# Attention probabilities turned by transposing DMAs instead of TensorE transposes, with some products of values moved later

## The reference, cut to what matters

```
s = einsum('bqhd,bkhd->bhqk', q, k) * scale        # scores, masked
p = softmax(s, axis=-1)
y = einsum('bhqk,bkhd->bqhd', p, v)                # product of values
```

## Time and profile before

| | us |
|---|---|
| median of 3 runs | 1520.27 (1520.24 to 1520.3) |
| the profiled execution | 1520.18 |
| its span, first to last instruction | 1518.1 |
| TensorE busy | 1510.1 |
| VectorE busy | 637.6 |
| ScalarE busy | 475.0 |
| GpSimd busy | 1027.0 |

### The profile page before, as it was taken

The page is one execution under the profiler, slowest core; times in us unless marked ns, Lnnn a source line. Parts: engine busy times, 40 slices in busy tenths (PEclk is TensorE's granted clock), DMA queues, the critical chain, the costliest instruction groups (busy, mean ns, idle before and its releaser), DMA issues.

```text
span 1518.1 us, 32667 instructions
## 1 busy us (share of the span) xinstructions
PE 1510.1 (99%) x13880; PEld 1174.1 (77%) x13882; DVE 637.6 (42%) x1509; ACT 475.0 (31%) x1243; POOL 1027.0 (68%) x565
## 2 busy tenths in 40 slices
PE   9999999999999999999999999999999999999998
PEld 7666888898666866669889966669888889888885
DVE  4332385445332333315844533325454535464532
ACT  3221163413221132204541232213443313343322
POOL 6976667667767677775586677773858565648653
PEclk9999999999999999999999999999999999999999
DMA  9665554455655565555545465664455554546551
GB/s 390 224 212 200 183 189 173 167 179 217 210 200 198 192 237 207 194 202 196 175 167 186 176 236 194 204 211 156 161 198 193 183 195 155 177 150 239 170 192 56
DMA packets 42625, 293.96 MB, mean 194 GB/s; under 512 B 4720, under 2 KB 5232, under 8 KB 8688
## 3 DMA queue, kind: packets, MB, share of 16 engines
q1 hardware_dynamic: 41760, 290.83, 54.5%
q10 hardware_dynamic: 720, 1.04, 0.2%
HBM read 290.81 MB, written 1.05 MB: 192 GB/s over the span
## 4 chain that ended last, share of the span: by engine, by line
PE 97%; DVE 2%; ACT 1%; issue 0%; DVEq 0%
PE ps L774 26%; PE ps L656 15%; PE ps L657 15%; PE ps L658 15%; PE ps L775 13%; PE ps L675 1%; PE ps L677 1%; PE ps L676 1%; PE ps L869 1%; PE ps L889 1%; ACT ps L1308 1%; PE ps L823 0%; PE ps L734 0%; PE ps L824 0%; PE ps L825 0%; PE ps L851 0%
## 5 line engine op out<-in xcount | busy, mean ns | idle before, releaser
L626 POOL TENSOR_TENSOR w_low<-ring 128x1024 f16<-128x1024 f32 (+1 forms) x544 | 1008.2, 1880 | 379.0 <-DMA ring<-in_w 378.7
L656 PE MATMUL ps<-hP,ring 128*128 128x256 f16 (+1 forms) x1936 | 469.1, 257 | 0.8 <-DVE work L1957 0.4
L657 PE MATMUL ps<-hP,ring 128*128 128x256 f16 (+1 forms) x1936 | 468.9, 257 | 0.0
L658 PE MATMUL ps<-hP,w_low 128*128 128x256 f16 (+1 forms) x1936 | 468.8, 257 | 0.0
L774 PE MATMUL ps<-hP,ring 128*128 128x512 f16 x1280 | 416.3, 380 | 0.0
L775 PE MATMUL ps<-hP,w_low 128*128 128x256 f16 x1280 | 349.2, 273 | 0.0
L774 PEld LDWEIGHTS ps<-hP,ring 128*128 128x128 bf16 x1280 | 125.0, 98 | 151.5 <-issue 0.4
L656 PEld LDWEIGHTS ps<-hP,ring 128*128 128x128 bf16 x1936 | 189.9, 98 | 23.3 <-issue 5.4
L657 PEld LDWEIGHTS ps<-hP,ring 128*128 128x128 bf16 x1936 | 189.2, 98 | 15.6
L658 PEld LDWEIGHTS ps<-hP,w_low 128*128 128x128 f16 x1936 | 189.2, 98 | 15.5
L774 PE MATMUL ps<-work,ring 128*128 128x512 f16 x528 | 171.8, 380 | 0.0
(11 more groups left out here) (277 smaller groups left out, 1740.8 us busy)
## 6 DMA issues: line engine op xcount, KB each, us to landing
ring<-in_w SPq DMA_DIRECT2D x261, 1024.0 KB, 4.8
ring<-in_w SPq DMA_DIRECT2D x12, 512.0 KB, 3.6
con<-in_const SPq DMA_DIRECT2D x1, 2812.0 KB, 18.3
gm<-in_gm SPq DMA_DIRECT2D x2, 1024.0 KB, 17.8
ring<-in_w SPq DMA_DIRECT2D x2, 768.0 KB, 4.9
ring<-in_w SPq DMA_DIRECT2D x2, 560.0 KB, 5.4
ring<-in_w SPq DMA_DIRECT2D x2, 544.0 KB, 3.5
xT<-in_x SPq DMA_DIRECT2D x3, 256.0 KB, 4.1
```

Of the source, the lines that this page charges most:

```text
L626: nc.gpsimd.tensor_tensor(w_low[:, c % SLOTS, a:b], ring[:, c % SLOTS, a:b], w_high[:, c % SLOTS, a:b], ALU.subtract).then_inc(split.by((c ...
L656: nc.tensor.matmul(bank, w_high[:, slot, a:a + m], rhs(k, 0), start=(k == 0), stop=False)
L657: nc.tensor.matmul(bank, w_high[:, slot, a:a + m], rhs(k, 1), start=False, stop=False)
L658: mm = nc.tensor.matmul(bank, w_low[:, slot, a:a + m], rhs(k, 0), start=False, stop=(k == kt - 1))
```

## The change: what it does

`normalise` writes the rounded 16-bit probabilities straight into `probsP` (head, high or low part, column) in SBUF. A new function `lows` on VectorE forms the low parts from PSUM by eight instructions, one per head and half of the queries, and raises `probs_ready` after every two heads. `turn` moves from TensorE to ScalarE's queue: for each two heads it waits for `probs_ready` and issues one transposing DMA from `probsP` to `probsTP`, both parts at once. TensorE's 12 transposes per unit, `copy_turned` and `low_turned` go, with the semaphores `turned`, `turned_copied` and `turned_low`. `mix` waits for the two DMAs of its unit.

In the second mixers the product of "s" moves behind bk0 to bk3 and bv0, bv1; that of "w" behind kcmp, vcmp and merge(0,0), and the scores of "b" behind one more merge; the product of "b" moves on by two merge tiles in all. All later steps of these mixers keep their order and stand two merge tiles further on, up to the stick-breaking product, and the last stage's turn of the stream is one tile later. On ScalarE and VectorE the same steps move along; dk1 is taken ahead of the exponentials of "w" and ahead of the last `rope`.

```diff
+        probsP = work[:, 0:4 * PACK].bitcast(F16).rearrange("p (h s n) -> p h s n", h=4, s=2)
...
-                def turn(s, u):
-                    pe.wait_ge(*probs_ready.at((s, u)))
-                    for h in range(4):
-                        for a in range(0, PACK, P):
-                            mm = nc.tensor.transpose(ps[:, 4 + h, a:a + P], probs[:, h, a:a + P], const("ident"))
-                    mm.then_inc(turned.by((s, u)), 1)
...
-                    pe.wait_ge(*turned_low.at((s, u)))
+                    pe.wait_ge(probs_turned, 32 * in_turn[s, u])
...
-                    turn(s, "s")
                     gemm("dq", 1), gemm("dk", 0)
-                    mix(s, "s", "cvg", lambda t, h: c_vg_h[:, t, 0:HD], lambda t, h: c_vg_l[:, t, 0:HD])
                     for n in range(4):
                         gemm("bk", n)
                     gemm("bv", 0), gemm("bv", 1)
+                    mix(s, "s", "cvg", lambda t, h: c_vg_h[:, t, 0:HD], lambda t, h: c_vg_l[:, t, 0:HD])
...
-                    turn(s, "w")
                     gemm("hid", 0), gemm("hid", 1), gemm("dg", 1)
-                    mix(s, "w", "cvg", lambda t, h: c_vg_h[:, t, HD:P], lambda t, h: c_vg_l[:, t, HD:P])
                     gemm("kcmp", 0), gemm("vcmp", 0)
                     merge(0, 0)
+                    mix(s, "w", "cvg", lambda t, h: c_vg_h[:, t, HD:P], lambda t, h: c_vg_l[:, t, HD:P])
+                    merge(0, 1)
                     pe.wait_ge(*mixed_taken.at((s, "w")))
                     pe.wait_ge(*taken(s, ("bq", 3)))
                     scores(s, "b", lambda h: b_qT[:, h, :], lambda h: b_kT[:, h, :])
-                    merge(0, 1), merge(0, 2), merge(0, 3)
-                    turn(s, "b")
-                    merge(0, 4), merge(0, 5)
+                    for n in range(2, 8):
+                        merge(0, n)
                     mix(s, "b", "bv", lambda t, h: b_v_h[:, t, h * HD:h * HD + HD],
                         lambda t, h: b_v_l[:, t, h * HD:h * HD + HD])
-                    merge(0, 6)
+                    merge(1, 0)
...
-                def copy_turned(s, u):
-                    act.wait_ge(*turned.at((s, u)))
-                    nc.scalar.activation(probsTP[:, :, 0, :], ps[:, 4:8, 0:PACK], ACT.Copy).then_inc(turned_copied.by((s, u)), 1)
+                def turn(s, u):
+
+                    for half in range(2):
+                        act.wait_ge(*probs_ready.at((s, u, half)))
+                        hs = slice(2 * half, 2 * half + 2)
+                        act.dma_start_transpose(probsTP[:, hs, :, :].rearrange("p h s (a q) -> p (h s a) q", q=P),
+                                                probsP[:, hs, :, :].rearrange("p h s n -> p (h s n)")).then_inc(probs_turned, 16)
...
-                        ins = nc.vector.tensor_tensor(probs[:, :, a:b], ps[:, 4:8, a:b], r, ALU.mult)
-                    ins.then_inc(probs_ready.by((s, u)), 1)
-
-                def low_turned(s, u):
-                    dve.wait_ge(*turned_copied.at((s, u)))
-                    nc.vector.tensor_tensor(probsTP[:, :, 1, :], ps[:, 4:8, 0:PACK], probsTP[:, :, 0, :], ALU.subtract
-                                            ).then_inc(turned_low.by((s, u)), 1)
+                        ins = nc.vector.tensor_tensor(probsP[:, :, 0, a:b], ps[:, 4:8, a:b], r, ALU.mult)
+                    chain.link(ins)
+
+                def lows(s, u):
+                    for h in range(4):
+                        for t, (a, b) in enumerate(HALVES):
+                            ins = nc.vector.scalar_tensor_tensor(probsP[:, h, 1, a:b], ps[:, 4 + h, a:b], sums[:, t, h:h + 1],
+                                                                 probsP[:, h, 0, a:b], ALU.mult, ALU.subtract)
+                        if h % 2:
+                            ins.then_inc(probs_ready.by((s, u, h // 2)), 1)
```

More of the change, by code:

```diff
@@ L479, in build @@
         exps_ready = signal("exps_ready", units)
[L480 to L483, removed]
+        probs_ready = signal("probs_ready", [(s, u, half) for s, u in units for half in range(2)])
+        in_turn = {unit: i + 1 for i, unit in enumerate(units)}
         v_split = signal("v_split", [(s, u) for s in mixers for u in (("v",) if s in MIX_A else ("av", "cvg", "bv"))])
@@ L1141, in mixer_b @@
                     mm.then_inc(cmp_turned.by(s), 1)
-                    merge(1, 1)
+                    merge(1, 3)
                     pe.wait_ge(*cmp_copied.at(s))
@@ L1148, in mixer_b @@
                     mm.then_inc(cmp_mixed.by(s), 1)
-                    merge(1, 2)
+                    merge(1, 4)
                     pe.wait_ge(*y_low.at((s, "c")))
@@ L1155, in mixer_b @@
                     mm.then_inc(stick_scores.by(s), 1)
-                    for n in range(3, 8):
+                    for n in range(5, 8):
                         merge(1, n)
-                    merge(2, 0)
+                    merge(2, 0), merge(2, 1), merge(2, 2)
                     pe.wait_ge(*stick_low.at(s))
@@ L1169, in mixer_b @@
                     mm.then_inc(stick_sums.by(s), 1)
-                    merge(2, 1), merge(2, 2), merge(2, 3)
+                    merge(2, 3), merge(2, 4), merge(2, 5)
                     pe.wait_ge(*stick_probs.at(s))
                     mix_values(lambda t, h: d_v[:, t, h * HD:h * HD + HD]).then_inc(stick_mixed.by(s), 1)
-                    for p in range(20, 32):
-                        if s == LAST_STAGE and p == 22:
+                    for p in range(22, 32):
+                        if s == LAST_STAGE and p == 23:
                             pe.wait_ge(*y_low.at((s, "d")))
@@ L1378, in mixer_a @@
                     take("va", 0)
-                    copy_turned(s, 0)
+                    turn(s, 0)
                     take("va", 1)
@@ L1385, in mixer_a @@
                         take("ga", n)
-                    copy_turned(s, 1)
+                    turn(s, 1)
                     act.wait_ge(*variance.at(s))
@@ L1494, in mixer_b @@
                     gate("ag", 0)
-                    copy_turned(s, "a")
+                    turn(s, "a")
                     gate("ag", 1)
@@ L1503, in mixer_b @@
                     take("dq", 0)
-                    copy_turned(s, "s")
+                    turn(s, "s")
                     take("dq", 1)
@@ L1535, in mixer_b @@
                     nc.scalar.activation(ps[:, 4:8, 0:PACK], ps[:, 4:8, 0:PACK], ACT.Ln, bias=1.0).then_inc(stick_ln.by(s), 1)
-                    for p in range(12, 18):
-                        if p == 15:
+                    for p in range(14, 20):
+                        if p == 17:
                             act.wait_ge(*stick_sp.at(s))
@@ L1542, in mixer_b @@
                     nc.scalar.activation(probsT, ps[:, 4:8, 0:PACK], ACT.Exp).then_inc(stick_probs.by(s), 1)
-                    merge(2, 2), merge(2, 3)
+                    merge(2, 4), merge(2, 5)
                     y_parts(3)
-                    for p in range(20, 24):
-                        if s == LAST_STAGE and p == 22:
+                    for p in range(22, 24):
+                        if s == LAST_STAGE and p == 23:
                             for i in range(4):
@@ L1863, in mixer_a @@
                     normalise(s, 0)
-                    low_turned(s, 0)
+                    lows(s, 0)
                     y_parts(0)
@@ L1874, in mixer_a @@
                     normalise(s, 1)
-                    low_turned(s, 1)
+                    lows(s, 1)
                     dve.wait_ge(*deviation.at(s))
@@ L2026, in mixer_b @@
                     low("qc", 1), low("kc", 0)
+                    lows(s, "a")
                     for t in range(TT):
@@ L2040, in mixer_b @@
                     normalise(s, "s", gates_c(1))
+                    lows(s, "s")
                     gate("bg", 1)
@@ L2080, in mixer_b @@
                     biggest(s, "b")
-                    merge(0, 1)
+                    merge(0, 2)
                     normalise(s, "b")
-                    merge(0, 2), merge(0, 3)
-                    low_turned(s, "b")
-                    merge(0, 4), merge(0, 5)
+                    lows(s, "b")
+                    for n in range(3, 8):
+                        merge(0, n)
                     dve.wait_ge(*mixed.at((s, "b")))
```

59 lines of the change are left out of this document (29 added, 30 removed), and 2 rows, old and new, of the table DVE_TAKES.

## The result

The changed kernel takes 1585.36 us (median of 4 runs, 1581.80 to 1589.69) against 1520.26 for the kernel before on the same chip: 1.043 times as long, 95% interval 1.0417 to 1.0442. The forecast was 1505.2 with a range to 1530, and a chance of 0.24 for slower. What happened is rival 2, at its place and with its sign, but larger than it said.

A forecast was written before the change was run, and what follows sets the result against it. TensorE was taken as the bound, busy 1510.1 of 1518.1 us. Turns removed 17.0, less 1.4 for moved products and 0.6 for late transfers, gave 15.0 and 1520.2 - 15.0 = 1505.2 us; range 1502.5 to 1530.

The forecast's parts named there:

- rival 2: At TensorE's wait for the product of values: transfers so late that the kernel is slower than before; chance 0.21.
- The turns, 17.0: On TensorE: removing 144 transposes saves 8 x 1.30 + 4 x 1.64 = 17.0 us, all on the path.
- The lows, 2.8 per unit: On VectorE: eight added operations per unit take 2.8 us, bounds 2.4 and 3.3, hidden in first mixers.
- the windows of "s", "w" and "b": Second mixers: time a unit can wait before TensorE reaches the product of values; 4.7, about 6 and 7.0 us.
- The moved products, 1.4: Second mixers: lost cover stalls TensorE 0.45 us at the first merge tile and 0.25 in "s", each twice; 1.4.
- L = 4.8: DMA queues: from ScalarE's readiness to both transposing DMAs landed, 4.8 us; stalls of 0.6 us in all.
- The 0.37: DMA engines: share of the first-mixer window in which they were read as busy with weights, 0.37.
- costed at nothing: ScalarE's queue: being held at its two DMA issues costs nothing, bounds 0 and 1 us per unit.
- break-even of L = 6.6: At the product of values: at about 6.6 us landing time, stalls of 15.8 eat the whole gain of 15.6.
- 1549 for L = 9: At the product of values: with 9 us landing time, stalls of 44 us give a kernel time of 1549 us.
- The far case: DMA queues: each 128x128 block turned as its own transfer, 46 us per unit, about 2000 us; chance 0.03.
- The weights' slack, 17 us: Six-slot weight ring: 17 us are left before a delayed load is felt, so its cost is nothing.

The follow-up runs named there:

- filled: The changed kernel, with small matmuls into an unused corner of PSUM filling TensorE's waits: 1580.14 us, ratio 1.0386.
- order_only: The changed kernel with all turns back on TensorE, keeping the second mixers' products one or two tiles later: 1521.65 us, ratio 1.0009.
- b_not_held: four_kinds_sooner without holding weight loads ahead of "b": 1510.77 us, ratio 0.9937.
- s_too: b_not_held with "s" turned by DMAs too, its load held and its product behind bv1: 1509.57 us, ratio 0.9935.
- a_by_pe_too: b_not_held with "a" turned by TensorE as well: 1513.39 us, ratio 0.9956.
- stand_back: The changed kernel, with SyncE holding one weight load and those behind it in each unit until its turned probabilities land: 1522.58 us, ratio 1.0015.
- four_kinds: The changed kernel with DMAs only in units 0, 1, "a", "b"; "s", "w" on TensorE at old places; loads held one earlier than in stand_back: 1527.41 us.
- four_kinds_sooner: four_kinds with ScalarE issuing the turns ahead of one take or gate: 1520.66 us, ratio 0.9999.
- half_bytes: The changed kernel with one head per DMA instead of two, part of the result left out: 1535.55 us, ratio 1.0100.
- nothing_held: b_not_held without any holding of weight loads: 1535.15 us, ratio 1.0098.
- w_by_pe: The changed kernel with the turn of "w" alone on TensorE: 1567.03 us, ratio 1.0307.
- nobody_waits: The kernel before plus transposing DMAs whose results nobody uses, beside weight loads and behind the last store: 1544.07 us in one run.

## Why the prediction failed, point by point

The profiled runs, by one sum (us; waits from TensorE's list, 1.9 before; turns by 1.30 and 1.64; filled: the fillers' 44.4 counted as waits). The last column is no part of the sum: it is the time that TensorE worked in stretches with a granted clock of 0.50.

| kernel | span | turns | waits | remainder | worked at 0.50 |
|---|---|---|---|---|---|
| order_only | +1.6 | 0 | +1.7 | -0.1 | 0 |
| b_not_held | -9.2 | -11.1 | +2.0 | -0.1 | 0 |
| s_too | -10.5 | -13.7 | +3.3 | -0.1 | 0 |
| a_by_pe_too | -6.8 | -8.5 | +1.0 | 0.7 | 0 |
| stand_back | +1.6 | -17.0 | +15.4 | 3.2 | 3.4 |
| four_kinds | +7.3 | -11.1 | +14.9 | 3.5 | 6.6 |
| four_kinds_sooner | +0.7 | -11.1 | +7.8 | 4.0 | 6.4 |
| half_bytes | +11.6 | -17.0 | +22.7 | 5.9 | 10.6 |
| nothing_held | +15.1 | -11.1 | +19.7 | 6.5 | 13.1 |
| w_by_pe | +46.6 | -13.7 | +45.9 | 14.4 | 28.1 |
| after | +64.9 | -17.0 | +63.8 | 18.1 | 36.9 |
| filled | +53.0 | -17.0 | +63.6 | 6.4 | 10.2 |

1. **The turns, 17.0: right.** Where nothing waits long the sum closes within 0.1 us, once 0.7 (first four lines). Taking the distance to the next start, and not the matmuls' listed durations, was right.
2. **The lows, 2.8 per unit: right**, 2.69 measured, and hidden in the first mixers. But the windows of "s", "w" and "b" were counted from the end of all eight, while the first DMA goes after four. In s_too the lows of "s" run from 1095.75 to 1098.44, the first DMA is issued at 1097.17 and the product starts at 1103.34: 6.2 us where 4.7 was said. Most of the loss lay in the other six, 31.4 of the 38.8 us of waits.
3. **The moved products, 1.4: right in sum**, placed a little wrong: in order_only dg1 costs 0.6 a time where 0.45 was said, and bk3 nothing where 0.25 was said. That bk3 waits 1.25 a time after the change (L975) is ScalarE's hold in "s", a matter of point 6.
4. **L = 4.8: the step that failed.** "I take 4.8, the row of the 1024 KB load, for a hardware-queue transfer beside the same traffic." That row times a transfer of another kind. Page and runs show what differs: the DMA queue of the turns moved 3136 packets and 0.79 MB per unit, 251 bytes each, and they took (3.8% - 0.2%) x 1583 / 12 = 4.7 us of all sixteen engines; at the weight loads' own rate (54.5% x 1518 us for 290.83 MB, 2.84 us per MB) they would take 2.2. To this came 1.45 us between the two issues: 5.6 on quiet engines (nobody_waits). And beside weight loads it about doubled once more, to 8.5 to 14.2 in the six units that the forecast hung on; with the loads held (stand_back) it was 5.5 to 6.8 there. The prediction had a bound there, 6.0, by doubling 1.8 us of transfer; both numbers under the doubling were those of plain loads.
5. **The 0.37 was one window's.** It was read at unit 0 alone, and with TensorE on time. Ahead of "w" the DMA share before the change was already near full, as a window of the kernel before shows that the prediction did not read:

```profile
1125.00:1135.00 10.00, 9.89 (x177) 8.84 (x176) 5.08 (x9) 4.67 (x9) 3.99 (x3) 1.00 0.94 345
```

6. **ScalarE's hold, "costed at nothing": the second failed term.** An issue of 12 blocks takes 1.4 us of ScalarE at best, about 1.7 on the median of b_not_held and 9.84 amid a burst of loads. The work hidden behind it was named for "s"; that hid1's take stands behind the same issues in "w" was not followed. It cost 2 x 10 us of waiting; w_by_pe gave back 18.3.
7. **The clock was no term at all.** The remainder is next to nothing where TensorE never worked at the lower level (first four lines of the table). Elsewhere it follows the last column, at about half of it: 6.5 for 13.1, 14.4 for 28.1, 18.1 for 36.9. That is what the lower level costs by rows: in the changed kernel two products start 0.11 us apart before the wait at 255.3 and 0.20 behind it, so 36.9 us of work there are, by estimate, 17 to 18 us lost. So nearly all of the 18.1 is the lowered clock. One to two us stay open in stand_back, four_kinds_sooner and filled. As a share of the waits the remainder is 0.21 to 0.51; a stall costs more than it lasts once the granted clock falls in it.
8. **Rival 2** had the place and the sign. Its break-even of L = 6.6 was too generous: in stand_back the six short windows have an L of 5.5 to 6.8, 6.1 on average, and wait 1.0 a time (5.9 in all), and nothing is gained any more; the hold in "w" (5.2) and the remainder (3.2), which it left out, are the difference. Its 1549 for L = 9 failed on points 4, 6 and 7. With L = 11 its own sum gives 6 x 6.2 + 2 x 6.3 + 2 x 5 + 2 x 4 = 68, near the waits' 63.8, but by another way: "w" and "b" waited for ScalarE or not at all. The range's lower end, 1502.5, is 0.7 below its own reason: 1520.2 less all 17.0 is 1503.2.
9. **The far case**, one block after the other, is excluded: 24 blocks in 5.5 us alone. The Trainium skill's 1309 ns for a block (VectorE: DVE Perf Modes, The three transpose paths) would make 31 us of them by estimate; the trace disagrees. The Trainium skill's advice on the same page (Rules for kernel authors), TensorE for such a block where PSUM will do, held while the weight loads ran on (nothing_held, 15 us slower than before) and not where they were held (b_not_held, 9.5 faster). The Trainium skill's nine tenths of a copy's rate (Advanced Engine Details and Errata, X-Bar Transpose) are not borne out either: 4.7 us of the engines against 2.2 for the same bytes as weight loads.
10. **The weights' slack, 17 us: right as far as it was tried.** Twelve holdings of 8.5 us on average, the longest 9.6, brought no wait for weights. It was the resource that the change should have used.

## What to carry to other kernels

Price a new transfer by one of its own kind, measured beside the traffic of its place, and price the issue on the engine that makes it: here a plain load's 4.8 us stood for 8.5 to 14.2, and nothing for up to 9.8. If a prefetch ring has slack, hold its next loads while a small transfer on the critical path runs (1535 us without, 1511 with), then look at what the burst that catches up collides with. Follow everything that stands behind an issuing instruction on its engine, in every stage in which it occurs, and count a stall of TensorE at more than its length once the granted clock falls in it: what TensorE then does at the lower level takes nearly twice as long.

## What the runs showed of the hardware

- **Transposing transfers are made of small packets**, 251 bytes on average for 128 x 1536 16-bit elements; alone 12 blocks land in 3.6 us and 24 in 5.5, beside 1 MB loads in 5.0 to 6.5 and 11.0 to 11.4.
- **Another queue's loads hold the issuing engine.** The same issue took 1.46 us on quiet engines and 9.84 with five weight loads issued around it, within 8 us, on SyncE's queue; with half the bytes still 8.87, at the second issue. A queue of its own does not protect the issuer.
- **Small VectorE operations slow down beside GpSimd.** tensor_tensor and tensor_scalar of 128x8 and 128x120, float32 from SBUF to SBUF, took 1.1 to 1.9 us while GpSimd split weights, 1.88 us apiece, and 0.17 and 0.29 otherwise, in b_not_held both within 5 us. The tensor_reduce operations of the same chain (0.28) were not slower in either kernel. That GpSimd is the cause follows from the coincidence and from b_not_held; neither engine was tried alone.
- **What the lower clock costs.** In ten stretches of the changed kernel with a granted clock of 0.50 TensorE worked 36.9 us, and the span holds 18.1 us that are neither waits nor turns; three kernels without such a stretch have -0.1 each, a fourth 0.7.
- **Spread.** The kernel before stays within 0.1 us of its median in the four runs beside the change, and the change within 4.4. Part of that goes with the clock: its four runs, from 1581.80 to 1589.69, have a mean granted clock from 0.982 down to 0.978. But s_too, with no long wait in its profile and a clock of 0.999 or 1.000 in every run, ranged from 1508.55 to 1514.30. Why isn't shown.
